# The first mixer's projections as three rounded products, its weights split by ScalarE and VectorE

## The reference, cut to what matters

```
mod = silu(c) @ ada_w + ada_b          # per layer 6*1024 values, for x and for ctx
h   = rmsnorm(x) * (1 + sc_m) + sh_m   # 512 tokens: x and ctx
p   = h @ w_in                         # 1024 x 2560: u, v, q, k, v'
a   = gelu(u) * (sgu_w @ rmsnorm(gelu(v)) + sgu_b)     # "SGU"
b   = neighbourhood / context attention(q, k, v')      # 8 heads
x   = x + g_m * (concat(a, b) @ w_out)                 # 1024 x 1024
x   = x + g_f * swiglu(rmsnorm(x) * (1 + sc_f) + sh_f) # dense, hidden 2816
```

## Time and profile before

| what | us |
|---|---|
| median of 3 runs | 2886.25 |
| the profiled execution | 2896.4 |
| its span, first to last instruction | 2894.6 |
| PE busy | 2686.7 (93% of the span) |
| DVE busy | 1904.4 (66%) |
| ACT busy | 1124.9 (39%) |
| mean granted TensorE clock | 0.961 of full |

### The profile page before, as it was taken

The page is one execution under the profiler, slowest core; times in us unless marked ns, Lnnn a source line. Parts: engine busy times, 40 slices in busy tenths (PEclk is TensorE's granted clock), DMA queues, the critical chain, the costliest instruction groups (busy, mean ns, idle before and its releaser), DMA issues.

```text
span 2894.6 us, 36210 instructions
## 1 busy us (share of the span) xinstructions
PE 2686.7 (93%) x13737; PEld 2161.1 (75%) x13737; DVE 1904.4 (66%) x2215; ACT 1124.9 (39%) x1422; POOL 51.7 (2%) x98
## 2 busy tenths in 40 slices
PE   7989899998997999978998978799999999999998
PEld 2445588886576998766998757688888888888886
DVE  4747656656045875344777263688887878788786
ACT  3123100002041001243101152577777777777775
POOL 1101000000000000000000000000000000000000
PEclk8999999999988999999999999799999999999999
DMA  8713344433213544311454402398988989898895
GB/s 346 306 38 139 123 147 145 149 133 110 87 59 136 185 178 145 109 59 66 168 181 144 147 30 88 121 376 327 366 335 327 375 326 376 318 374 326 327 375 208
DMA packets 88785, 598.59 MB, mean 207 GB/s; under 512 B 9728, under 2 KB 10752, under 8 KB 22016
## 3 DMA queue, kind: packets, MB, share of 16 engines
...
## 4 chain that ended last, share of the span: by engine, by line
PE 88%; DVE 5%; ACT 3%; issue 2%; DMA 1%; POOL 0%; DVEq 0%; ACTq 0%; POOLq 0%
PE bank L450 16%; PE bank L621 9%; PE bank L625 8%; PE bank L624 8%; PE bank L1519 7%; PE bank L1523 7%; PE bank L1522 7%; PE bank L464 4%; PE bank L1552 4%; PE bank L1555 4%; PE bank L1556 4%; PE bank L480 2%; PE bank L798 1%; ACT arena L815 1%; PE bank L1486 1%
## 5 line engine op out<-in xcount | busy, mean ns | idle before, releaser
L591 DVE TENSOR_TENSOR ring_part<-ring,arena_part 128x2048 fp32r<-128x2048 f32 x437 | 983.9, 2287 | 59.6 <-ACT arena_part L1783 55.2
L1783 ACT ACTIVATE arena_part<-ring 128x2048 fp32r<-128x2048 f32 x339 | 642.7, 1918 | 152.9 <-DMA ring<-in_stream 152.7
L621 PE MATMUL bank<-arena_part 128*128 128x256 f32 (+1 forms) x1584 | 510.8, 322 | 31.7 <-issue 24.4
L625 PE MATMUL bank<-arena_part,ring_part 128*128 128x256 f32 (+1 forms) x1584 | 507.4, 320 | 0.0
L1519 PE MATMUL bank<-arena_part 128*128 128x512 f32 x896 | 355.6, 397 | 3.3 <-issue 2.8
L1523 PE MATMUL bank<-arena_part 128*128 128x512 f32 x896 | 350.6, 391 | 0.0
L1522 PE MATMUL bank<-ring_part,arena_part 128*128 128x512 f32 x896 | 349.8, 390 | 0.0
L621 PEld LDWEIGHTS bank<-arena_part 128*128 128x128 f32 x1584 | 304.1, 192 | 59.4 <-issue 26.0
L624 PE MATMUL bank<-h_part,arena_part 128*128 128x256 f32 (+1 forms) x1056 | 338.9, 321 | 0.0
L450 PE MATMUL bank<-h_normed,ring 128*128 128x256 f32 (+1 forms) x1024 | 304.4, 459 | 20.7 <-issue 10.8
L625 PEld LDWEIGHTS bank<-arena_part,ring_part 128*128 128x128 f32 x1584 | 304.6, 192 | 21.0
...
## 6 DMA issues: line engine op xcount, KB each, us to landing
ring<-in_stream SPq DMA_DIRECT2D x515, 1024.0 KB, 4.8
arena<-in_ada_stream POOLq DMA_DIRECT2D x80, 512.0 KB, 4.6
...
arena<-in_c_rows POOLq DMA_DIRECT2D x2, 1024.0 KB, 7.9
arena<-in_ab_bias POOLq DMA_DIRECT2D x1, 2048.0 KB, 12.9
...
x_stream<-in_x_t POOLq DMA_DIRECT2D x1, 1024.0 KB, 14.3
x_stream<-in_ctx_t POOLq DMA_DIRECT2D x1, 1024.0 KB, 20.6
```

The costliest lines, as they stand in the source:

```text
L591: return nc.vector.tensor_tensor(low, value, high.bitcast(F32), ALU.subtract)
L621: m = nc.tensor.matmul(out_ap, w_high, high, start=start, stop=False)
L625: return nc.tensor.matmul(out_ap, w_low, high, start=False, stop=stop)
L1783: nc.scalar.activation(high, ring[:, where], ACT.Copy).then_inc(sem("moe_high"), 1)
```

## The change

- **In-projection** (10 slots) and **out-projection** (4 slots) of layer 0 go through `split_products` and `split_token_products`. Their slots are rounded by ACT (`slot_high_act`) and the low part is taken by DVE (`slot_low_dve`), into two alternating buffers. Slots are counted from `AB_AT` (the ninth slot of the stream): AB+0 to AB+9 are w_in, AB+10 to AB+13 are w_out. The token tiles of v and v' now accumulate in four banks at once, chunk by chunk. PE starts each group with a pair of outputs, so that every input chunk is used twice as it arrives.
- **Dense inputs split by chunks.** `rms_split_dve` and `shift_high_act` replace `rms_dve` and `split_input`: ACT writes scale-and-shift results already rounded, and DVE takes the low part of chunk c-1 after it has scaled chunk c. Layer 0's in-projection and all three dense FFN inputs use it (the third through `ln_dve(split=True)`).
- **The mixed input** of the out-projection is copied rounded by ACT and reduced by DVE after the attention.
- **Schedule of the chunks:** 24 instead of 32 in the in-projection (three per slot, between the lows, through a ring of 3 instead of 4), 8 instead of 12 in the out-projection, the rest in the FFN loop (9 instead of 6 per turn, 3 of them for both sides) and behind it.
- **Transfers:** x and ctx are issued on SP ahead of the ring's slots, no longer on POOL. The SGU weights and attention bias are issued after the last first chunk. The memset of `down_acc` goes from DVE to POOL, behind the second input split, and DVE waits for it ahead of the FFN.
- `products` with a `ready` also starts with a pair of outputs.

```diff
-ADA_FIRST = [(0, n) for n in range(16, 48)]
-ADA_OUT = [(1, n) for n in range(12)]
-ADA_LOOP = [(1, n) for n in range(16, 46)]
-ADA_REST = [(1, n) for n in (12, 13, 14, 15, 46, 47)]
+ADA_FIRST = [(0, n) for n in range(16, 40)]
+ADA_OUT = [(1, n) for n in range(7, 15)]
+LOOP_TWO, LOOP_ONE = 3, 6
+ADA_LOOP = [divmod(40 + LOOP_TWO * i + j, 48) if j < LOOP_TWO else (1, 16 + LOOP_ONE * i + j - LOOP_TWO)
+            for i in range(5) for j in range(LOOP_TWO + LOOP_ONE)]
+ADA_REST = [(1, n) for n in (15, 46, 47)]
 ADA_CHUNKS = ADA_FIRST + ADA_OUT + ADA_LOOP + ADA_REST
-FIRST_RING, LATE_RING = 4, 3
+FIRST_RING, LATE_RING = 3, 3
+AB_AT = SLOTS_ADA
...
+            pair = []
+            if ready:
...
+                for k in range(kc):
+                    ready(k)
+                    for n, b in enumerate(pair):
+                        m = nc.tensor.matmul(PS[b][:, 0:cols], both[:, (n * kc + k) * P:(n * kc + k + 1) * P], rhs(k),
+                                             start=k == 0, stop=k == kc - 1)
...
+        def slot_high_act(book, n, highs, fresh=False):
+
+            if not fresh:
+                book.eng.wait_ge(sem("slots_used"), n)
+            book.eng.wait_ge(sem(f"slot_landed{n % RING}"), 16 * (n // RING + 1))
+            nc.scalar.activation(highs[n % 2], ring[:, n % RING * SLOT:(n % RING + 1) * SLOT], ACT.Copy)\
+                .then_inc(sem("slot_rounded"), 1)
+
+        def slot_low_dve(book, n, highs):
+            at = slice(n % RING * SLOT, (n % RING + 1) * SLOT)
+            book.eng.wait_ge(sem("slot_rounded"), book.up("slot_rounded"))
+            low_dve(ring_part[:, at], ring[:, at], highs[n % 2]).then_inc(sem("slot_split"), 1)
...
+        def shift_high_act(book, l, m, sides, high):
             for c in range(DC):
+                for s in range(sides):
+                    t = slice(SEQ * s, SEQ * (s + 1))
+                    book.eng.wait_ge(sem("scaled"), book.up("scaled"))
+                    nc.scalar.activation(high[:, c, t], hv[:, c, t], ACT.Identity, bias=shift(l, m, c, s))\
+                        .then_inc(sem("in_high"), 1)
+
+        def rms_split_dve(book, l, m, sides, high=None, rooted=False):
+
+            high = in_high if high is None else high
+            if not rooted:
+                root_dve(book, SEQ * sides)
+            for c in range(DC + 1):
+                for s in range(sides):
+                    t = slice(SEQ * s, SEQ * (s + 1))
+                    if c < DC:
+                        nc.vector.scalar_tensor_tensor(hv[:, c, t], xv[:, c, t], scalev[:, l, m, c, s:s + 1],
+                                                       rstd[:, t], ALU.mult, ALU.mult).then_inc(sem("scaled"), 1)
+                for s in range(sides):
+                    t = slice(SEQ * s, SEQ * (s + 1))
+                    if c:
+                        book.eng.wait_ge(sem("in_high"), book.up("in_high"))
+                        ins = nc.vector.scalar_tensor_tensor(h_part[:, c - 1, t], hv[:, c - 1, t],
+                                                             shift(l, m, c - 1, s),
+                                                             high[:, c - 1, t].bitcast(F32), ALU.add, ALU.subtract)
+                if c:
+                    ins.then_inc(sem("in_split"), 1)
...
+        def split_products(book, w, n_out, high, low, cols, highs, ready="in_split"):
+
+            pair = []
+            for n in range(2):
+                pair.append(book.next_bank())
+                book.eng.wait_ge(free(pair[-1]), book.emptied())
+            for k in range(DC):
+                book.eng.wait_ge(sem(ready), book.up(ready))
+                for n, b in enumerate(pair):
+                    m = split_product(book, w, PS[b][:, 0:cols], high[:, k, 0:cols], low[:, k, 0:cols],
+                                      k == 0, k == DC - 1, tile=n * DC + k, highs=highs)
+                    if k == DC - 1:
+                        m.then_inc(full(b), 1)
+            w.t += TILES
+            more_split_products(book, w, n_out - 2, high, low, cols, highs)
...
+        def split_token_products(book, w, high, low, tiles, highs, n=2):
+
+            banks = []
+            for t in range(tiles):
+                banks.append(book.next_bank())
+                book.eng.wait_ge(free(banks[-1]), book.emptied())
+            per = DC // n
+            for k in range(DC):
+                r, j = w.t // TILES, k % per
+                if j == 0:
+                    book.eng.wait_ge(sem("slot_split"), book.up("slot_split"))
+                w_high = highs[r % 2][:, j * 512:(j + 1) * 512]
+                w_low = ring_part[:, r % RING * SLOT + j * 512:r % RING * SLOT + (j + 1) * 512]
+                for t, b in enumerate(banks):
+                    x_high, x_low = (x[:, k, t * P:(t + 1) * P] for x in (high, low))
+                    m = nc.tensor.matmul(PS[b][:, :], x_high, w_high, start=k == 0, stop=False)
+                    if j == 0 and t == 0:
+                        m.then_inc(sem("slots_used"), 1)
+                    nc.tensor.matmul(PS[b][:, :], x_high, w_low, start=False, stop=False)
+                    m = nc.tensor.matmul(PS[b][:, :], x_low, w_high, start=False, stop=k == DC - 1)
+                    if k == DC - 1:
+                        m.then_inc(full(b), 1)
...
-            products(bk, w, 4, h_all, TT, ready=h_ready(2))
-            token_products(bk, w, lambda k, t: hv[:, k, t * P:(t + 1) * P], 4)
-            products(bk, w, 8, h_all, TT)
-            token_products(bk, w, lambda k, t: hv[:, k, t * P:(t + 1) * P], 4)
+            split_products(bk, w, 4, ab_high, h_part, TT, ab_slot_high)
+            split_token_products(bk, w, ab_high, h_part, 4, ab_slot_high)
...
-            outs = attention_pe(bk, ab_steps())
-            pe.wait_ge(sem("sgu_ready"), bk.up("sgu_ready", 4))
-            out_products(h_all, 2, outs)
-            sum_pe(bk, "squared", lambda c: sqv[:, c, :], TT)
-            bk.up("h_ready", 16)
+            attention_pe(bk, ab_steps())
+            split_products(bk, w, DC, mixed_high, h_part, TT, out_slot_high, ready="mixed_split")
+            sum_pe(bk, "squared", lambda c: sq_out[:, c, :], TT)
...
+            slot_high_act(bk, AB_AT, ab_slot_high, fresh=True)
+            act.wait_ge(sem("mod_ready"), 1)
+            shift_high_act(bk, 0, 0, 2, ab_high)
+            slot_high_act(bk, AB_AT + 1, ab_slot_high, fresh=True)
             silu_rows(rows_first, 1)
             for g in range(4):
                 to(uT[:, g, :], ACT.Gelu_apprx_tanh)
+                if g == 1:
+                    slot_high_act(bk, AB_AT + 2, ab_slot_high)
+            slot_high_act(bk, AB_AT + 3, ab_slot_high)
+            slot_high_act(bk, AB_AT + 4, ab_slot_high)
             for t in range(4):
                 to(v_tok[:, t, :], ACT.Gelu_apprx_tanh)
             act.wait_ge(*bk.freed(bk.turn - 1))
+            slot_high_act(bk, AB_AT + 5, ab_slot_high)
             for t in range(4):
...
+                    slot_high_act(bk, AB_AT + 6, ab_slot_high)
+            for n in range(7, 10):
+                slot_high_act(bk, AB_AT + n, ab_slot_high)
+            act.wait_ge(sem("sgu_ready"), 4)
+            slot_high_act(bk, AB_AT + 10, out_slot_high, fresh=True)
+            slot_high_act(bk, AB_AT + 11, out_slot_high, fresh=True)
             attention_act(bk, ab_steps())
+            act.wait_ge(*bk.freed(bk.turn - 1))
+            for c in range(DC):
+                nc.scalar.activation(mixed_high[:, c, :], hv[:, c, :], ACT.Copy).then_inc(sem("mixed_high"), 1)
+            slot_high_act(bk, AB_AT + 12, out_slot_high)
             silu_rows(rows_late, 2)
+            slot_high_act(bk, AB_AT + 13, out_slot_high)
             bk.turn += DC
...
-            rms_act(bk, 0, 1, 2, last)
+            rms_split_act(bk, 0, 1, 2, last, sq_out)
...
+            slot_low_dve(bk, AB_AT, ab_slot_high)
+            rms_split_dve(bk, 0, 0, 2, ab_high, rooted=True)
+            slot_low_dve(bk, AB_AT + 1, ab_slot_high)
             bk.turn += 4 + 4
             dve.wait_ge(sem("c_rows_ready"), 1)
-            first_chunks(0, 20)
-
+            for n in range(2, 7):
+                first_chunks(3 * n - 6, 3 * n - 3)
+                slot_low_dve(bk, AB_AT + n, ab_slot_high)
...
-            first_chunks(20, 32)
+            first_chunks(15, 18)
+            slot_low_dve(bk, AB_AT + 7, ab_slot_high)
+            first_chunks(18, 21)
+            bk.turn += 4
+            for c in range(2):
+                to(kT[:, c, :])
+            slot_low_dve(bk, AB_AT + 8, ab_slot_high)
+            first_chunks(21, 24)
...
-            bk.turn += 4
-            for c in range(4):
+            for c in range(2, 4):
                 to(kT[:, c, :])
+            slot_low_dve(bk, AB_AT + 9, ab_slot_high)
             for t in range(4):
                 to(v_att[:, t, :])
             dve.wait_ge(sem("ab_landed"), 48)
...
                 dve.wait_ge(*bk.freed(bk.turn - 1))
```

(25 more changed lines are left out.)

221 lines of the change are left out of this document (137 added, 84 removed).

## The result

The changed kernel took **2856.63 us** (median of 4 runs, 2855.35 to 2857.26) against 2884.93 for the kernel before on the same chip: ratio 0.9892, 95% interval 0.988 to 0.9905, 28.3 us less. Repeated in a second batch it was 2854.69 against 2887.99 (ratio 0.9885, 0.9868 to 0.9901), 33.3 us less. The forecast was 2851.7 us, its own range 2847 to 2857.

A forecast was written before the change was run, and what follows sets the result against it. PE mostly bounds the first 309 us, with DVE and ACT sharing the chain around SGU and attention. Terms 23.3 + 4.9 + 1 + 2.7 + 2.7 = 34.6 us, from 2886.25 to 2851.7 us; own range 2847 to 2857.

The forecast's parts named there:

- steps 1, 3, 4: In-projection and SGU: product 0.681 us instead of 0.862; gain 25.2 us at the in-projection's end, 17.1 at attention's start.
- step 4: SGU and low parts ahead of attention: v' copies 2.6 us behind PE's end, not 0.7; gain down to 17.1 us.
- Rival (a): In-projection: DVE or ACT sets the pace, 10 us of gain go, 2862 us; chance 15%.
- Start: Kernel start: x and ctx loaded ahead, the sum no longer waits for squares; 0 to 2 us gained, taken 0.7.
- Attention: Layer 0's attention: 1 us lost to PE's clock, 1.4 us to the first mixed chunk's copy and subtraction before the out-projection.
- step 5: Out-projection: DVE decides, PE stalls 1.9 us for AB+12; 8.6 us gained of the 11.5 saved on PE.
- First feed-forward: Layer 0's FFN: 4.9 us gained by its input, 1 us by fewer chunks at the loop's end.
- Third: FFN of the second stack's layer 0: 2.7 us gained by its input, its scales standing as in layer 1.
- step 6: FFN inputs: 4.9 us gained in layer 0, 2.7 in layer 1, 2.7 in the second stack's layer 0.
- rival (c): In-projection: late chunks in the ring of 3 stop PE, 43 us lost, slower than before at 2895 us; chance 3%.
- step 3: In-projection: 25.2 us gained by its end; small constants hold chunk 13 up by 3 to 8 us, nothing counted.
- The rule weighed: DVE copies or casts in two-port mode lock out GpSimd's descriptors; moving slot casts to ACT can only help chunk transfers.

The follow-up runs named there:

- before again: The kernel before, unaltered, run once more for a second trace; 2889.29 us for its one run, beside 2888.31 for its others.
- two-products kernel: Changed kernel with one of the three products left out in the first mixer's in-projection (output not the reference's); 2849.14 us.
- the kernel with the silu first: Changed kernel with the late rows' load mark right behind the attention and their silu ahead of the out-projection's third slot's rounding; 2852.85 us.

## Why the prediction was right, and where its sizes were off

The forecast (34.6 us less, 2851.7 us) holds: faster, 28.3 us in one batch and 33.3 in the other, a time inside its own range of 2847 to 2857, near the upper end in the first (2856.63). Where it put the gains is right; that the total fits so well is luck, as the terms show. They are taken against before again and the mean of the two traces of the changed kernel:

- *Product price and the in-projection* (steps 1, 3, 4): 16.4 us without the start; 18.3 measured (154.65 to 136.34). TensorE is dense to the end and ends at 156.8 in the first trace, where 157.0 was put. The rest is step 4's copies of v': it put them wholly behind TensorE's end, but they begin at 154.82, and the SGU at 157.83, not 159.7. Rival (a) did not happen, but the two-products kernel shows its bound some 4 us away.
- *Start*: 0.7 put; 3 in these traces, within a scatter of 3. The fifth slot came 1.6 us later in the first trace, as feared. The sum behind it no longer waits, and takes 8.03 and 7.13 us, not 9.68.
- *Attention*, up to the out-projection's first product: 2.4 us worse put (1 for the clock, 1.4 for the mixed input); 0.9 and 1.2 measured.
- *Out-projection* (step 5): 8.6 put, 5.5 and 6.6 measured (62.80 to 57.29 and 56.16). The chain of rows, silu, chunks and third slot was the right one, the stall 2.37 for 1.9; VectorE's last residual ended at T+53.5, not T+51.5 (T is 224.74 here). The step that failed is "PE does the sum of the first seven chunks in that time": TensorE ended its products at T+49.5 (T+47.9 in the second trace), not T+45.5, with part of the stretch at the low clock (0.93 from 225 to 288), and did the whole sum behind them. Without the stall, in the kernel with the silu first, the products end at T+45.2: the stall costs more than its 2.37 us.
- *First feed-forward*: 5.9 put, 10.3 measured. The input gave 4.87 (10.97 to 6.10 from the reciprocal to the first product), as put. The end, put at 1 us, gave 3.2 in the first traces up to the residual, of which 1.25 is TensorE's last wait for a slot (2.61 to 1.36); and 1.7 is the sum of squares at a higher clock (8.80 to 7.11), for which nothing was put.
- *Second*: 2.7 put, 3.2 measured. *Third*: 2.7 put, 1.35 measured, and only 0.76 of it by the edit to its input. TensorE's gap ahead of it did shrink, from 6.35 to 4.14 us, but step 6 took layer 1's scales for its model, and here ScalarE's eight shifts and their table load follow and delay the first silu. Moving them behind gave 0.55 us; the rest stays open.
- *Stages marked * in the table*: nothing put. The paired products are worth nothing there, as put (232.42 before, 232.58 and 232.62 with them where the clock runs alike). But the stages gained 3.1 in the second mixer and lost 3.1, 4.8 and 1.6 in the three others: 6.4 us lost in all. This is the term that was missing: the prediction put these stages at nothing because their code is the same. The gain and the loss of 3.1 belong together: in the table, wherever the second mixer takes 214.7 or more, the third takes 244.1 at most, and where the second takes 212.0 to 212.7, the third takes 246.8 to 247.0. What is left over is the fourth mixer and the experts. The other stages gave 41 us, not 34.6.

Shown is that the losses in the third and fourth mixer do not come from the stage's own code: the fourth takes 232.6 or 237.2 us by an edit to the feed-forward ahead of it, the third 244.1 or 246.9 by leaving out products a thousand microseconds earlier. The slower course has the lower granted clock each time (0.89 against 0.91 from the fourth mixer's first reciprocal to its next); for the experts' 1.6 us the mean clock shows nothing, 0.98 in both. Whether the clock makes the loss or goes along with it, and what sets its course from such distance, stays open.

The excess of the profiled execution of before (2896.4) over its median was carried over unchanged. For the median that did no harm, since only differences enter it; for the span it was wrong, 2860 put and 2854.8 measured, since 3.9 us of the excess in the attention, 3.0 in the second mixer and 1.8 in the experts are gone in before's second trace. The two errors, a loss of 6.4 left out and gains sized 6.5 too small, cancelled by luck.

Of the signs, the attention's first score came at 170.35 for 172, the stall was 2.37 us for 2, the reciprocal started at 282.03 for 286, and the gaps before the three feed-forwards shrank by 4.9, 2.2 and 2.2 us for 5, 3 and 3. TensorE's products ended only 4 us ahead of VectorE's last residual, not 6. The sign of rival (c), a wait for a chunk beyond 3 us, did show: 6.1 us, once, at 104.84, of the size that step 3 had estimated for the small constants. TensorE did not notice it, and (c) did not come. The rule weighed was not tested: all chunk transfers issued in the out-projection took 0.53 us each, and none was issued beside a cast.
